# A decoder layer on one core: where the block sums of the gate and up weights are made, and who computes the two gate columns in front of the tokens

## What is computed

```python
def _conv_glu(h, w_gate, w_up, ffn_conv_w, ffn_conv_b, w_down):
    gate = _causal_dwconv(h @ w_gate, ffn_conv_w) + ffn_conv_b
    return (jax.nn.silu(gate) * (h @ w_up)) @ w_down
```

## Time and profile before

| what | value |
|---|---|
| runs of the kernel | 3242.87, 3245.88, 3246.95 us |
| profiled execution, its own time | 3256.48 us |
| its span | 3254.8 us |
| mean granted clock of TensorE | 0.941 |
| DMA, mean over the span | 130 GB/s |

### The profile page before, as it was taken

How to read it: one execution, slowest core, us unless ns; L and a number is a source line. 1 busy time by engine, 2 the same in 40 slices (tenths; PEclk the granted TensorE clock), 3 DMA queues, 4 the chain that set the end, 5 groups by cost and what they waited for, 6 DMA issues and landing times. The chain is left out here.

```text
span 3254.8 us, 49226 instructions
## 1 busy us (share of the span) xinstructions
PE 2873.8 (88%) x19127; PEld 2499.6 (77%) x19127; DVE 1810.0 (56%) x2752; ACT 1186.9 (36%) x2197; POOL 1110.3 (34%) x1195
## 2 busy tenths in 40 slices
PE   6797848996899979999299679999999999699999
PEld 6797748996788868888287568888878888588887
DVE  3123833443355467776579466665697777524444
ACT  3223722221444455554233243333343333323312
POOL 2602740001777500000254255555566666200000
PEclk9998978998799989999699889999999999899999
DMA  6953673223444131210357533223353333545554
GB/s 235 364 168 92 170 235 127 89 75 90 91 107 101 41 109 56 75 56 20 129 169 230 177 127 96 92 93 98 94 173 107 105 97 104 192 125 190 172 169 146
DMA packets 413470, 421.97 MB, mean 130 GB/s; under 512 B 38282, under 2 KB 335766, under 8 KB 412214
## 3 DMA queue, kind: packets, MB, share of 16 engines
q1 hardware_dynamic: 379534, 306.64, 31.2%
q10 hardware_dynamic: 21384, 67.36, 6.3%
q0 software_dynamic: 12320, 44.80, 4.1%
HBM read 258.18 MB, written 160.55 MB: 129 GB/s over the span
## 5 line engine op out<-in xcount | busy, mean ns | idle before, releaser
L2836 PE MATMUL fu_pM<-fu_us_hi,fu_w_hi 128*128 128x512 f32 x1232 | 488.6, 397 | 35.9 <-DVE fu_us_lo L2669 35.9
L2836 PE MATMUL fu_pM<-fu_us_lo,fu_w_hi 128*128 128x512 f32 x1232 | 486.4, 395 | 0.0
L2836 PE MATMUL fu_pM<-fu_us_hi,fu_w_lo 128*128 128x512 f32 x1232 | 486.0, 394 | 0.0
L2836 PEld LDWEIGHTS fu_pM<-fu_us_hi,fu_w_hi 128*128 128x128 f32 x1232 | 235.6, 191 | 88.6 <-issue 29.0
L2836 PEld LDWEIGHTS fu_pM<-fu_us_hi,fu_w_lo 128*128 128x128 f32 x1232 | 235.4, 191 | 50.1
L2836 PEld LDWEIGHTS fu_pM<-fu_us_lo,fu_w_hi 128*128 128x128 f32 x1232 | 235.5, 191 | 48.7
L3071 PE MATMUL fd_pM<-fd_bs_hi,fd_a_hi 128*128 128x512 f32 x616 | 241.5, 392 | 27.6 <-DVE fd_bs_lo L3003 22.4
L3071 PE MATMUL fd_pM<-fd_bs_hi,fd_a_lo 128*128 128x512 f32 x616 | 240.6, 391 | 0.0
L3071 PE MATMUL fd_pM<-fd_bs_lo,fd_a_hi 128*128 128x512 f32 x616 | 240.4, 390 | 0.0
L2583 ACT ACTIVATE fu_w_hi<-fu_sw 128x512 fp32r<-128x512 f32 x176 | 111.3, 633 | 323.6 <-PE fu_pM L2836 262.5
L2998 DVE TENSOR_TENSOR fd_a_lo<-fd_a_lo,fd_a_hi 128x1408 fp32r<-128x1408 f32 x56 | 91.0, 1626 | 235.9 <-ACT fd_a_hi L2954 235.9
(11 more groups left out here) (403 smaller groups left out, 7174.2 us busy)
## 6 DMA issues: line engine op xcount, KB each, us to landing
fd_a_lo<-scr_gs ACTq DMA_DIRECT2D x56, 704.0 KB, 4.6
fu_w_raw<-in_w_gate SPq DMA_DIRECT2D x22, 1024.0 KB, 5.5
fu_w_raw<-in_w_up SPq DMA_DIRECT2D x22, 1024.0 KB, 5.3
scr_gs<-fu_sg SPq DMA_DIRECT2D x88, 256.0 KB, 2.7
scr_gs<-fu_acc SPq DMA_DIRECT2D x66, 256.0 KB, 2.5
pj_wd<-in_w_down POOLq DMA_DIRECT2D x11, 1024.0 KB, 12.0
scr_td<-pj_td POOLq DMA_DIRECT2D x11, 1024.0 KB, 8.6
fd_b_raw<-scr_td SPq DMA_DIRECT2D x44, 256.0 KB, 5.1
```

The source lines that it names most:

```text
L2836: p = pe.matmul(bank(2 * n + m, i)[:, :], a[:, k, :], x[:, k, :], start=(k == 0 and n_pass == 0), stop=(k == HALVES_K - 1 and n_pass == 2))
```

## The change

Three things. In attention GpSimd, behind each group's output store (groups 0 to 14), does three of 44 units: half of the rows of a column pair of gate or up are loaded by two DMAs of 256 KB, the four sums are formed on 128 x 256 tiles, and 512 KB are stored to a new scratch tensor `ws`. One tile `fw` holds the input, one tile `fs` the output. In the gate/up stage GpSimd forms no weight sums any more; SyncE loads them (1 MB a phase) right behind the raw weights, into two buffers `sw`. And the gate columns are computed by VectorE: for each of 8 row blocks k and both positions t the raw weights times the position's value of each partition are added up in `hacc`, 16 operations of 256 columns; TensorE only adds over the partitions, with 4 products against a column of ones, now after unit 5 instead of unit 2. ScalarE's copy of them moves from step 4 to step 6.

```diff
@@ stage_attention, GpSimd
+            def load_unit(x):
+                j, m, half = x // 4, x // 2 % 2, x % 2
+                w = A["w_up" if m else "w_gate"][0].rearrange("(q k p) n -> p q k n", p=P, q=2)
+                for q in range(2):
+                    pool.dma_start(fw[:, q, :, :], w[:, q, 2 * half:2 * half + 2, 2 * j * P:2 * j * P + 2 * P]).then_inc(fw_loaded, 16)
+
+            def weight_sums(x):
+                j, m, half = x // 4, x // 2 % 2, x % 2
+                a11, a21, a12, a22 = (fw[:, q, :, row * P:row * P + P] for q in range(2) for row in range(2))
+                pool.wait_ge(fw_loaded, 32 * (x + 1))
+                if x:
+                    pool.wait_ge(fs_stored, 16 * x)
+                pool.tensor_tensor(fs[:, 0, :, :], a21, a22, ALU.add).then_inc(fs_step, 1)
+                pool.tensor_tensor(fs[:, 2, :, :], a11, a21, ALU.subtract).then_inc(fs_step, 1)
+                pool.wait_ge(fs_step, 4 * x + 1)
+                pool.tensor_tensor(fs[:, 1, :, :], fs[:, 0, :, :], a11, ALU.subtract).then_inc(fs_step, 1)
+                pool.wait_ge(fs_step, 4 * x + 3)
+                pool.tensor_tensor(fs[:, 3, :, :], a12, fs[:, 1, :, :], ALU.subtract).then_inc(fs_step, 1)
+                pool.wait_ge(fs_step, 4 * x + 4)
+                if x + 1 < UNITS_F:
+                    load_unit(x + 1)
+                pool.dma_start(S["ws"][j, m, :, :, 2 * half:2 * half + 2, :], fs[:, :, :, :]).then_inc(fs_stored, 16)
+
+            load_unit(0)
             for n, (h, g) in enumerate(ORDER):
...
+                for x in range(PER_GROUP * n, min(PER_GROUP * (n + 1), UNITS_F)):
+                    weight_sums(x)
...
+            pool.wait_ge(fs_stored, 16 * UNITS_F)
@@ stage_gate_up, SyncE, load_w
-                    sp.wait_ge(combined, 4 * (2 * n + m - 1))
                     if m == 0 and halo_set(n - 1):
-                        sp.wait_ge(halo_done, n)
+                        sp.wait_ge(halo_step, HALO * KD * n)
...
+                sp.dma_start(sw[m][:, :, :, :], S["ws"][j, m, :, :, :, :]).then_inc(s_loaded[m], 16)
@@ stage_gate_up, GpSimd: weights(n, m) with its four operations and waits goes
@@ stage_gate_up, ScalarE
-                    act.wait_ge(combined, 4 * ph + int(STRASSEN[i][1][1]))
+                    act.wait_ge(s_loaded[m], 16 * (n + 1))
...
-                    if m == 0 and i == 4:
+                    if m == 0 and i == 6:
                         before(n)
@@ stage_gate_up, VectorE
+        HALO_AT = {1: (0, 1, 2), 2: (3, 4), 3: (5, 6), 4: (7,)}
...
+            def halo_sums(n, ks):
...
+                    dve.wait_ge(raw_loaded[0], 16 * (n + 1))
+                for k in ks:
+                    for t in range(HALO):
+                        u = head[:, k, t:t + 1]
+                        if k == 0:
+                            m = dve.tensor_scalar(hacc[:, t, :], w_raw[0][:, k, :], u, None, ALU.mult)
+                        else:
+                            dve.wait_ge(halo_step, HALO * (KD * n + k - 1) + t + 1)
+                            m = dve.scalar_tensor_tensor(out=hacc[:, t, :], in0=w_raw[0][:, k, :], scalar=u,
+                                                         in1=hacc[:, t, :], op0=ALU.mult, op1=ALU.add)
+                        m.then_inc(halo_step, 1)
...
+                        if i in HALO_AT and halo_set(n):
+                            halo_sums(n, HALO_AT[i])
@@ stage_gate_up, TensorE, halo_products
+                pe.wait_ge(halo_step, HALO * KD * (n + 1))
...
                 for row in range(2):
-                    for k in range(KD):
-                        p = pe.matmul(bank(2 * n + 1, 0)[:, HALO * row:HALO * row + HALO], w_raw[0][:, k, row * P:row * P + P],
-                                      head[:, k, :], start=(k == 0), stop=(k == KD - 1))
+                    for t in range(HALO):
+                        p = pe.matmul(bank(2 * n + 1, 0)[:, HALO * row + t:HALO * row + t + 1], hacc[:, t, row * P:row * P + P],
+                                      ones[:, :], start=True, stop=True)
...
-                        if m == 0 and i == 2 and halo_set(n):
+                        if m == 0 and i == 5 and halo_set(n):
                             halo_products(n)
```

More of the change, by code:

```diff
@@ L1710, in stage_attention @@
         mask = r.sb("mask", [P, P])
+        fw = r.sb("fw", [P, 2, 2, 2 * P])
+        fs = r.sb("fs", [P, 4, 2, P])
         pS = [r.ps(f"pS{i}", [P, 512]) for i in range(NPS)]
@@ L1724, in stage_attention @@
         stored = r.sems("stored")
+        fw_loaded, fs_step, fs_stored = r.sem("fw_loaded"), r.sem("fs_step"), r.sem("fs_stored")
+        UNITS_F = 4 * PAIRS
+        PER_GROUP = -(-UNITS_F // (NG - 1))
         block = ctx.enter_context(nc.Block())
@@ L2402, in stage_gate_up @@
         w_raw = [r.sb(f"w_raw{i}", [P, KD, 2 * P]) for i in range(2)]
-        sw = r.sb("sw", [P, 4, HALVES_K, P])
+        sw = [r.sb(f"sw{i}", [P, 4, HALVES_K, P]) for i in range(2)]
         w_hi = [r.sb(f"w_hi{i}", [P, HALVES_K, P], F32R) for i in range(RING)]
@@ L2409, in stage_gate_up @@
         head = r.sb("head", [P, KD, HALO])
+        hacc = r.sb("hacc", [P, HALO, 2 * P])
+        ones = r.sb("ones", [P, 1])
         halo = r.sb("halo", [P, FT, HALO])
@@ L2419, in stage_gate_up @@
         u_loaded, u_half, u_ready = r.sems("u_loaded", UNITS_7), r.sem("u_half"), r.sem("u_ready")
-        raw_loaded, combined, w_half, w_ready = r.sems("raw_loaded"), r.sem("combined"), r.sem("w_half"), r.sem("w_ready")
+        raw_loaded, s_loaded, w_half, w_ready = r.sems("raw_loaded"), r.sems("s_loaded"), r.sem("w_half"), r.sem("w_ready")
         w_ready_pool = r.sem("w_ready_pool")
-        done, halo_done, halo_out, halo_kept = (r.sem(x) for x in ("done", "halo_done", "halo_out", "halo_kept"))
+        done, ones_made, halo_step, halo_done, halo_out, halo_kept = (r.sem(x) for x in ("done", "ones_made", "halo_step", "halo_done", "halo_out", "halo_kept"))
         m1_out, u2_made, u3_made, v_made = (r.sem(x) for x in ("m1_out", "u2_made", "u3_made", "v_made"))
@@ L2439, in operand @@
             name = STRASSEN[i][1]
-            return sw[:, int(name[1]) - 1, :, :] if name[0] == "S" else quads(m)[name]
+            return sw[m][:, int(name[1]) - 1, :, :] if name[0] == "S" else quads(m)[name]
         def bank(ph, i):
             return pM[(UNITS_7 * ph + i) % BANKS]
+        HALO_AT = {1: (0, 1, 2), 2: (3, 4), 3: (5, 6), 4: (7,)}
         def halo_set(n):
@@ L2523, in _ @@
             make_identity(pool, ident, id_made)
[L2525 to L2537, removed]
+            pool.memset(ones[:, :], 1.0).then_inc(ones_made, 1)
             def products(n):
@@ L2557, in _ @@
             for n in range(SETS):
-                weights(n, 0)
                 for i in POOL_SPLITS:
                     split(2 * n, i)
-                weights(n, 1)
                 if n:
@@ L2691, in make_u3 @@
                 dve.tensor_tensor(u3[:, :], bank(ph, 4)[:, :], u2[:, :], ALU.add).then_inc(u3_made, 1)
+            def halo_sums(n, ks):
+                if ks[0] == 0:
+                    if n:
+                        dve.wait_ge(halo_done, n)
+                    else:
+                        dve.wait_ge(consts, 48)
+                    dve.wait_ge(raw_loaded[0], 16 * (n + 1))
[4 more added lines that the diff above has]
+                            m = dve.tensor_scalar(hacc[:, t, :], w_raw[0][:, k, :], u, None, ALU.mult)
+                        else:
+                            dve.wait_ge(halo_step, HALO * (KD * n + k - 1) + t + 1)
+                            m = dve.scalar_tensor_tensor(out=hacc[:, t, :], in0=w_raw[0][:, k, :], scalar=u,
+                                                         in1=hacc[:, t, :], op0=ALU.mult, op1=ALU.add)
+                        m.then_inc(halo_step, 1)
             def gate_c11(n):
@@ L2840, in halo_products @@
             def halo_products(n):
+                pe.wait_ge(halo_step, HALO * KD * (n + 1))
                 if n == 0:
+                    pe.wait_ge(ones_made, 1)
                     pe.wait_ge(taps_ready, 1)
@@ L3095 @@
     "h2": (LP, D), "u2T": (P, KD, LP), "tT": (P, 2 * KD, LP),
-    "gs": (7, P, 8, PAIRS, P), "td": (4, PAIRS, P, 512),
+    "ws": (PAIRS, 2, P, 4, KD // 2, P), "gs": (7, P, 8, PAIRS, P), "td": (4, PAIRS, P, 512),
 }
```

## The result

The change makes the kernel slower: 3282.74 us (median of 4 runs, 3278.27 to 3290.24) against 3246.41 us (4 runs, 3242.87 to 3249.48), a ratio of 1.0115 with a 95% interval of 1.0091 to 1.0138. The forecast was 3214 us, with a range up to 3280. The profiled execution of after took 3290.24 us with a span of 3288.5.

What follows compares the result with a forecast made beforehand. TensorE's own queue was taken to bound gate/up, with room on GpSimd in attention. Gate/up -44 us (39 + 2 + 3) and attention +12 gave -32 us, from the median 3245.88 to 3214 us; range 3202 to 3246, whole 3194 to 3280.

Steps and rivals of the forecast that it cites:

- U = 8.4 us: Length of one GpSimd unit in attention: operations 2.93 us, waits and issues 1.75, landing of its store 3.7.
- the formula: Attention's delay: 38 U - 307.5 us, or 44 U - 366.3 where GpSimd never waits; forecast cost 12 us.
- rival (b): GpSimd sets attention's length and the kernel is slower; at units of 10 us, +30 us, 3276 us; chance 0.25.
- is in time: In attention, GpSimd's store two groups back, awaited by VectorE's output normalisation, was to land without causing a wait.
- rival a: In attention, stores land in 3.2 us or less, GpSimd keeps up, the whole 44 us stay: 3202 us; chance 0.2.
- No other slowing of attention: Attention was costed only for late GpSimd units, 12 us; slowing by its sums or transfers was costed at nothing.
- The narrow block: Gate/up, TensorE's 8 gate-column instructions instead of 32: 1.0 us a set, clock staying up, 39 us gained in sets 1 to 10.
- VectorE's column sums at nothing: Gate/up: 16 operations at 0.42 us, 6.7 us a set, with 2.9 us of slack before TensorE asks; new wait costed at nothing.
- rival (c): Gate/up: clock still falls, 13 us less gained, or TensorE waits some 1 us a set; 3227 or 3224 us; chance 0.12.
- Taking the sums from GpSimd in this stage frees nobody on the path: Gate/up: removing GpSimd's weight sums was given no gain on TensorE's path, since TensorE is busy without a gap.
- Sets 0, 10 and 11: Gate/up: 2 us gained in set 0, 3 in set 11; set 10 counted within the 39 us of sets 1 to 10.
- The 14 us: Gate/up: the shortfall against the forecast gain of 44 us, where 30.0 us were measured.

Runs made afterwards that it cites:

- e4_store_first: The changed kernel with each unit's store issued ahead of the next unit's two loads, one buffer each way as before: 3290.86 us, ratio 1.0136.
- e9_two_inputs_early: The changed kernel with two input tiles in attention and VectorE's column sums one step earlier in the set: 3224.16 us, ratio 0.9925.
- e11_sums_no_transfers: Changed kernel with two input tiles and earlier column sums, all sums in attention kept, loads and stores for the first two units alone: 3225.61 us, ratio 0.9922.
- e6_sums_only: Kernel before with the block sums moved to attention, two buffers each way, gate columns left on TensorE: 3272.64 us, ratio 1.0082.
- e1_columns_only: Kernel before with the gate columns alone moved to VectorE, GpSimd's weight sums still in the gate/up stage: 3282.79 us, ratio 1.0108.

## Why the prediction was wrong, point by point

- **The unit in attention: the step that failed.** "U = 8.4 us" measured 9.81. The parts: four operations 3.08 us (2.93 forecast; means 746, 786, 791 and 757 ns), waits and issues some 1.8 (1.75), and from the store's issue to the next unit 4.92 on average (3.7). Even the quiet units were above the forecast: the last 15, behind the last of SyncE's loads in the stage (issued at 1474.54), are 8.94 us long, 4.22 of it from the store's issue on. With these alone the formula gives 38 x 8.94 - 307.5 = 32 us, an estimate. What I had no term for are the units whose store meets SyncE's loads of queries, keys and values. After the issue at 1403.76 the next unit starts 8.04 us later, with the DMA engines at 0.91 from 1404 to 1408; of the 43 such times 14 are over 5 us, and in 11 of these 14 such a load is in flight. A landing time taken from a quiet row is a floor, where each store has to be waited for, not a mean.
- **The formula around it held.** At U = 9.81 GpSimd never catches up, and 44 U - 366.3 = 65.3 us; the last output store came 62.2 us later, attention was 65.7 longer. The result is rival (b), which had a chance of 0.25. What chose between it and the forecast was the landing almost alone, 1.22 of the 1.41 us by which U was short; rival (b) had put a part on operations stretched by a fifth, and they were stretched by a twentieth. That the output normalisation "is in time" hung on U = 8.4 as well: at 9.81 it waits 30.1 us.
- **"All hidden" (rival a).** The rule of the Trainium skill ("DMA: Bandwidth & Descriptors", Anatomy of one DMA) was worked out to an estimate of 3.2 us for the store. The trace agrees for a store issued first: 3.1 us in e4_store_first, 3.2 with two buffers. It does not hold for one behind two loads on the same queue, 4.1 us.
- **No other slowing of attention: wrong, by 14 to 21 us**, as e9_two_inputs_early and e11_sums_no_transfers show. It is hidden in the changed kernel, where the chain sets the length anyhow, and is all that is left once the chain is short. The Trainium skill ("GPSIMD Engine Reference", Key points) states the sharing that does it. I used it for the operations on GpSimd, in one sentence, and dismissed it since VectorE's large operations read PSUM. Those were in fact not touched (688 ns); the query, key and value splits were.
- **The narrow block: right.** 1.0 us forecast; 1.05 us, and the clock stays at 1.00. Where TensorE does not wait, a set takes 39.03 us against 39.1 forecast.
- **VectorE's column sums at nothing: wrong by 7 us.** In sets 1 to 10 the first two of the 16 operations (one tile as input) take 0.34 us each, ten of the others 474 ns and four 1.51 us, which makes 11.5 us instead of 6.7; the slack was "2.9 us", so the excess of 4.8 less 2.9 would be a wait of 1.9 us. It is 0.70 in sets 1 to 10. This is rival (c), about 1 us a set. The row I took the price from reads PSUM; the new operation reads SBUF twice. That alone costs little, 474 ns against 421: most of the excess is in the four that run beside GpSimd.
- **"Taking the sums from GpSimd in this stage frees nobody on the path": wrong in what it left out.** Sums alone give nothing there (e6_sums_only, +8 us), as the sentence says. But columns alone cost 32 us (e1_columns_only), and both together gain 30. The sums had to go for VectorE to be fast enough (40 of its operations at 1.5 us instead of 74), so that the parts of this change cannot be priced one by one.
- **Sets 0, 10 and 11.** Set 0: 2 us gained forecast, 0.5 lost (61.72 us against 61.27), for the block waits 8.52 us for VectorE behind the token splits, the last of which begins 23 us behind the first product where it began 17 us behind it. Set 11: 3 forecast, 2.0 measured (47.52 against 49.54). But 1.70 us of waiting for the same tokens moved to the end of set 10, so that hardly anything is gained. The 14 us are 2.5 of set 0, 10 x 0.86 + 1.9 = 10.5 of sets 1 to 10 and 1.0 of set 11.

The sum with the measured terms is -30.0 + 65.7 = +35.7 us; the medians differ by 36.3.

## What to carry to other kernels

Before giving idle GpSimd work in a stage, write its unit as a chain (loads, operations, store, wait) and price the landing in the busiest moments, not in the quiet ones; where the next unit waits for the last one's store, a second input tile costs nothing in time and can be worth more than the whole idea (here 56 us of the median). Then look for VectorE operations with two SBUF inputs beside it, in both stages: their price is to be taken from a row with the same kind of operands and the same neighbour. Two edits that share an engine are to be tried apart and together, since here, with two buffers in attention, the sums alone lose, the columns alone lose, and the pair gains.

## What the runs showed that I had not expected

- More than 40 MB of extra DMA traffic in attention's window, at a mean share of 0.53 instead of 0.18, left the stage's length unchanged at 414.0 us, though SyncE's loads of `at_v` landed later (4.7 us against 4.2).
- The same VectorE operation on 128 x 256 with both tiles in SBUF took either 0.47 us or, beside a GpSimd operation, some 1.5 us, and nothing in between. Its mean follows from how many of the 154 meet one: 743 ns with 40 (GpSimd's products and splits only), 969 with 74 (its weight sums as well), 1039 with 84 (moved to the earlier gaps there). A split of 128 x 512 with both inputs in SBUF took up to 1.97 us against 0.69.
- Of two loads of 256 KB and a store of 512 KB issued together on one queue, what is issued first lands after 3.1 to 3.3 us and what stands behind it after 4.1 to 4.4, in either order.
